# Two layer norms of a decoder layer, taken from sums and squares instead of transposes, and an up projection fed two tiles at a time

## The chip, the cores and the metric

The kernel runs on one core of a Trainium2 chip. The metric is the time of one execution on the device in microseconds (us). TensorE (PE) multiplies; VectorE (DVE), ScalarE (ACT) and GpSimd (POOL) do the elementwise work; SyncE (SP) issues most of the DMAs. Three runs of the kernel before took 1439.5 to 1440.29 us, median 1439.64.

## The reference

One decoder layer in fp32, for one prompt of 256 rows and eight sequences of four new rows each: 288 rows in all, model width 2048 (16 tiles of 128), FFN width 5504 (43 tiles).

```
shift1, scale1, gate1, shift2, scale2, gate2 = split(silu(c) @ w_ada + b_ada)
proj  = (x * (1 + scale1) + shift1) @ w_in            # q, k, v, u_a, v_a
mixed = concat(rms_norm(gated group), rms_norm(attention group))
x     = layer_norm(ALPHA * x + gate1 * (mixed @ w_out), ln1_g, ln1_b)
up    = (x * (1 + scale2) + shift2) @ w_up            # 86 tiles, then a causal conv of width 3
ff    = (silu(a) * b) @ w_down
y     = layer_norm(ALPHA * x + gate2 * ff, ln2_g, ln2_b)
# layer_norm(x): mu = mean(x); var = mean((x - mu)^2); (x - mu) * rsqrt(var + eps) * g + b
```

## The kernel before, in words

Everything lies with features on the partitions: xT holds x as 16 tiles of 128 features by 288 rows. So a layer norm's mean and variance run over partitions and tiles.

Weights stream through a ring of four slabs of 512 KB (raw). ScalarE copies a slab, rounded, to wH (`hi`, L920) and VectorE takes the remainder wL = raw - wH (`lo`, L1276). Activations are split in the same way (hH, hL), and each product is three matmuls (`products`, L444 to L446), 24 per slab. The semaphores split_done (slab ready) and used (slab consumed) order this; a slab is split three ahead of its use (AHEAD). Each engine's order is written out by hand, and each executes its list strictly in order, SyncE's queue of loads too.

The modulation (w_ada) is another stream: ada slabs in a ring of eight, multiplied in bursts of four between product slabs (`ada_next`, L460), copied by ScalarE (adaS, L932), transposed (`ada_turn`, L501) and added into modT by VectorE (`unit_finish`, L1290, L1494 to L1496). The last unit, U_SC2B, gives scale2 for the upper half of the tiles; its 16 ada slabs stand in the first norm.

Output projection, second half: four groups g of four output tiles, four slabs each (PSUM banks 0 to 3). When group g is done, `residual(g)` on VectorE adds gate times product to xT into S4 (L1649, L1650, L1654), and gives the banks back. ScalarE copies S4 to xT (`copy_sum`, L1149). TensorE transposes S4 into three banks (`turn_rows`, L750, 12 transposes), one group later, within the product loop, and VectorE takes bn_stats of the rows (L1660). After group 3, `normalise` aggregates, ScalarE takes the root (L1156), VectorE builds six diagonal matrices DG (L1677), and `spread_rows` multiplies ones by DG (L760) so that each row's 1/sd and -mean/sd stand on all partitions; they are copied to RN (L1158, L1682). `centre` applies them to four tiles at a time (L1688, L1689). In the first norm, per four tiles: H2 = x * scale2 + shift2 (ScalarE L1180 for the prompt, VectorE L1715, L1716 for the samples), hH (L1185), hL (L1722), and ScalarE's `affine` (L1166), which turns xT into the norm's output for the residual of the next norm. (ln1_g and ln1_b are folded into scale2 and shift2.)

Up phase: groups of eight slabs (`up_group`); each waits h2_ready for the four tiles that it reads. The first 32 slabs run in a loop of two with ada bursts (the last gate). Down projection: the last of three phases has groups of five and a half slabs, with the same residual, turn_rows and statistics. In the second norm VectorE centres tiles 0 to 11 and GpSimd tiles 12 to 15 (L1955, L1957), ScalarE applies g and b (L1166), and stores four tiles at a time (L1261).

## Time and profile before

| | us |
|---|---|
| median of three runs | 1439.64 |
| profiled execution | 1441.33 |
| its span | 1439.7 |
| TensorE busy | 1379.4 (96%) |
| VectorE busy | 843.0 (59%) |
| ScalarE busy | 571.5 (40%) |
| GpSimd busy | 109.6 (8%) |

The span runs from the first to the last instruction that the profiler saw; the execution's own time is 1.6 us longer. Busy shares are means over stages with different limits. Matmuls overlap in the pipeline, so a stretch in which TensorE is busy all the time isn't one at its peak. An fp32 matmul (not fp32r) is counted as two instructions, one per pass.

### The profile page before, as it was taken

How to read it: one execution, taken by the hardware profiler on the slowest of the kernel's cores; microseconds unless marked ns; L12 is line 12 of the kernel's file. 1: busy time of each engine (PE TensorE's matmuls, PEld its weight loads, DVE VectorE, ACT ScalarE, POOL GpSimd, SP SyncE). 2: the span in 40 equal slices, each digit the busy share in tenths (PEclk: the TensorE clock that was granted, in tenths of full speed). 3: DMA queues.
4: the chain of work that ended last, by engine and by line, in shares of the span. 5: the costliest groups of instructions: out<-in, count | busy, mean ns of one | idle time of the engine just before them, and what ended most of it. 6: DMA issues, size and time to landing. Idle time of an engine off the chain costs nothing.

```text
span 1439.7 us, 29195 instructions
## 1 busy us (share of the span) xinstructions
PE 1379.4 (96%) x11366; PEld 1307.1 (91%) x11366; DVE 843.0 (59%) x1375; ACT 571.5 (40%) x831; POOL 109.6 (8%) x252
## 2 busy tenths in 40 slices
PE   6999999999999998999999999999999999999992
PEld 5998888899788876989999999999999999999992
DVE  2476546558765456565667454675665445657555
ACT  3533222353533327443444333444444333444333
POOL 1000000003221000010101000010110000101002
PEclk9999999999999999999999999999999999999996
DMA  9989998974786985866554545445455444454621
GB/s 379 374 328 389 342 337 305 344 264 149 274 294 254 352 311 224 323 249 248 176 169 146 181 160 162 163 145 187 146 172 165 159 162 159 165 170 146 198 89 66
DMA packets 89183, 324.86 MB, mean 226 GB/s; under 512 B 10574, under 2 KB 10574, under 8 KB 88721
## 3 DMA queue, kind: packets, MB, share of 16 engines
q1 hardware_dynamic: 81216, 294.69, 57.5%
q0 software_dynamic: 6880, 24.10, 4.8%
q10 hardware_dynamic: 1008, 4.98, 0.9%
q8 instruction: 56, 0.92, 0.3%
q14 instruction: 23, 0.18, 0.0%
HBM read 318.05 MB, written 5.67 MB: 225 GB/s over the span
## 4 chain that ended last, share of the span: by engine, by line
PE 91%; DVE 4%; ACT 3%; issue 1%; DMA 1%; SPq 0%; ACTq 0%; DVEq 0%
PE ps L444 28%; PE ps L446 27%; PE ps L445 27%; PE ps L460 5%; ACT xT L1166 1%; DMA adaY<-w_ada 1%; PE ps L750 1%; PE ps L552 1%; DVE wL L1276 1%; DVE xT L1689 1%; DVE xT L1688 1%; ACT wH L920 1%; ACT H L1180 1%; PE ps L622 0%; PE ps L760 0%
## 5 line engine op out<-in xcount | busy, mean ns | idle before, releaser
L1276 DVE TENSOR_TENSOR wL<-raw,wH 128x1024 fp32r<-128x1024 f32 x372 | 448.7, 1216 | 375.9 <-ACT wH L920 373.2
L920 ACT ACTIVATE wH<-raw 128x1024 fp32r<-128x1024 f32 x372 | 389.5, 1053 | 602.5 <-PE ps L446 576.9
L444 PE MATMUL ps<-hL,wH 128*128 128x288 f32 x2016 | 603.5, 299 | 6.9 <-DVE hL L1314 4.0
L446 PE MATMUL ps<-hH,wH 128*128 128x288 f32 x2016 | 601.0, 298 | 0.0
L445 PE MATMUL ps<-hH,wL 128*128 128x288 f32 x2016 | 600.6, 298 | 0.0
L444 PEld LDWEIGHTS ps<-hL,wH 128*128 128x128 f32 x2016 | 381.5, 189 | 20.5 <-issue 8.9
L445 PEld LDWEIGHTS ps<-hH,wL 128*128 128x128 f32 x2016 | 381.1, 189 | 0.5 <-issue 0.5
L446 PEld LDWEIGHTS ps<-hH,wH 128*128 128x128 f32 x2016 | 380.2, 189 | 0.0
L444 PE MATMUL ps<-ffL,wH 128*128 128x288 f32 x688 | 204.4, 297 | 0.4 <-DVE xT L1769 0.3
L445 PE MATMUL ps<-ffH,wL 128*128 128x288 f32 x688 | 203.0, 295 | 0.0
L446 PE MATMUL ps<-ffH,wH 128*128 128x288 f32 x688 | 202.4, 294 | 0.0
L1455 DVE TENSOR_TENSOR proj<-ps,proj 128x288 f32<-128x288 f32 x160 | 71.0, 455 | 105.8 <-PE ps L446 105.3
L444 PEld LDWEIGHTS ps<-ffL,wH 128*128 128x128 f32 x688 | 128.9, 187 | 1.6 <-DVE xT L1769 1.5
L446 PEld LDWEIGHTS ps<-ffH,wH 128*128 128x128 f32 x688 | 129.6, 188 | 0.0
L445 PEld LDWEIGHTS ps<-ffH,wL 128*128 128x128 f32 x688 | 129.2, 188 | 0.0
L444 PE MATMUL ps<-mix,wH 128*128 128x288 f32 x256 | 80.0, 313 | 8.5 <-DVE xT L1541 4.3
L445 PE MATMUL ps<-mix,wL 128*128 128x288 f32 x256 | 77.2, 302 | 0.0
L446 PE MATMUL ps<-mix,wH 128*128 128x288 f32 x256 | 77.1, 301 | 0.0
L1933 POOL COPY E<-U 128x4 f32 (+1 forms) x44 | 9.0, 204 | 754.3 <-ACT U L1201 754.3
L444 PEld LDWEIGHTS ps<-mix,wH 128*128 128x128 f32 x256 | 49.7, 194 | 14.4 <-issue 9.5
L460 PE MATMUL ps<-ada,cT 128*32 128x256 f32 x832 | 51.7, 390 | 0.0
L445 PEld LDWEIGHTS ps<-mix,wL 128*128 128x128 f32 x256 | 49.9, 195 | 0.0
(230 smaller groups left out, 982.2 us busy)
## 6 DMA issues: line engine op xcount, KB each, us to landing
raw<-w_up SPq DMA_DIRECT2D x168, 512.0 KB, 3.5
ada<-w_ada SPq DMA_DIRECT2D x112, 512.0 KB, 6.2
raw<-w_down SPq DMA_DIRECT2D x84, 512.0 KB, 3.5
raw<-w_in SPq DMA_DIRECT2D x80, 512.0 KB, 7.9
adaX<-w_ada SPq DMA_DIRECT2D x40, 512.0 KB, 5.6
adaY<-w_ada SPq DMA_DIRECT2D x40, 512.0 KB, 7.4
raw<-w_out SPq DMA_DIRECT2D x32, 512.0 KB, 5.1
KV<-keys POOLq DMA_DIRECT2D x16, 512.0 KB, 5.8
```

Of the source, the lines that this page charges most:

```text
L444: nc.tensor.matmul(out, wH[:, w:w + P], rhs_lo(kk), start=start, stop=False)
L445: nc.tensor.matmul(out, wL[:, w:w + P], rhs_hi(kk), start=False, stop=False)
L446: mm = nc.tensor.matmul(out, wH[:, w:w + P], rhs_hi(kk), start=False, stop=stop)
L460: mm = nc.tensor.matmul(ps[32 * c:32 * c + 32, bank, 0:256], cT[:, 32 * k:32 * k + 32], src[:, 256 * c:256 * (c + 1)], start=(k == 0), sto ...
L552: mm = nc.tensor.matmul(b[:, lo:hi], ones[:, :], tile(proj, k0 + k, lo, hi), start=(k == 0), stop=(k == 7))
L750: mm = nc.tensor.transpose(b[0:n, t * P:(t + 1) * P], tile(S4, t, r * P, r * P + n), ident)
L920: nc.scalar.activation(wH[:, o:o + cols], raw[:, o:o + cols], ACT.Copy).then_inc(hi_done, 1)
L1166: y = nc.scalar.activation(tile(xT, k), tile(xT, k), ACT.Identity, scale=vec[:, scale_at + k:scale_at + k + 1], bias=vec[:, bias_at + k:bi ...
L1180: y = nc.scalar.activation(tile(H2, t, 0, SEQ), tile(xT, 4 * b4 + t, 0, SEQ), ACT.Identity, scale=modT[:, s:s + 1], bias=modT[:, c:c + 1])
L1276: vec_tt(wL[:, o:o + cols], raw[:, o:o + cols], wH[:, o:o + cols].bitcast(F32), ALU.subtract).then_inc(split_done, 1)
L1455: release(vec_tt(tile(proj, n), ps[:, k % 5, 0:ROWS], tile(proj, n), ALU.add), ("in", c, k))
L1688: steps.link(vec_tt(x, x, spread(RN[:, 0:1], [0, 4], [1, ROWS]), ALU.mult))
```

## The change

Both layer norms lose their transposes. After group 0's residual VectorE sums its four tiles per row (GS), one matmul of ones by GS (`centre_of`) gives the sum over the first 512 features on all partitions, and CM is that mean. It is subtracted from all tiles (`shift_group`), for groups 1 to 3 ahead of their residual. VectorE then gathers the sums (A1, `add_sum`) and the sums of ScalarE's squares (A2, `squares`, `add_squares`) of groups 0 to 2, one group later, by tensor_reduce over four tiles. `row_sums` on TensorE sums A1, A2, and the four tiles of group 3 and their squares over the partitions, with one moving column each: 10 x 3 matmuls, which give sums per row in six columns of a bank. From these come variance, root and mean in one column each; `spread_rows` multiplies that column, repeated 128 times as the stationary operand, by the identity, and `scaled` / `centred` read the result in PSUM. residual writes xT in place; S4 holds squares.

TensorE's order in the first norm: row_sums, eight ada slabs, spread_rows, four ada slabs, up slab 0, four ada slabs, up slab 1, the turn of U_SC2B, up slab 2 and on. The up phase waits for two tiles per slab; VectorE and ScalarE work in eight chunks of two tiles, with the splits of slabs S_UP+4 to S_UP+8 from chunk 3 on; the affine of xT moves behind, into slabs 8 to 15 of the up phase. The loop of two there is written out. In the second norm VectorE scales, ScalarE prepares WN = (-mean/sd) * g + b for each tile, VectorE forms x * g + WN, and SyncE stores two tiles at a time. GpSimd has no part in it. A one-column sqrt stands ahead of the last down phase.

```diff
+CM, _ = place("CM", [P, ROWS], over=o_cv)
+GS, _ = place("GS", [P, ROWS], over=o_cv + 4 * ROWS)
+A1, _ = place("A1", [P, ROWS], over=o_cv + 8 * ROWS)
+A2, _ = place("A2", [P, ROWS], over=o_cv + 12 * ROWS)
+TS, _ = place("TS", [P, 4 * SAMP], over=o_bd)
+WN, _ = place("WN", [P, T], over=o_h)
...
-    def turn_rows(g, ln):
...
+    def centre_of(ln):
+        pe.wait_ge(group_sum, ln + 1)
+        b = take(pe, ("centre", ln), 4)
+        fill(nc.tensor.matmul(b[:, 0:ROWS], ones[:, :], GS[:, :], start=True, stop=True), ("centre", ln))
+    def row_sums(ln):
+        pe.wait_ge(acc_ready, ln + 1)
+        b = take(pe, ("sums", ln), 5)
+        def add(src, at, first=False, last=False):
+            for r, lo in enumerate(ROW_BLOCKS):
+                mm = nc.tensor.matmul(b[:, at + r:at + r + 1], src[:, lo:lo + P], ones[:, 0:1], start=first and r == 0, stop=last and r == 2)
+            return mm
+        add(A1, 0, first=True)
+        add(A2, 3)
+        for t in range(4):
+            pe.wait_ge(d_ready, 7 * ln + 4 + t)
+            add(tile(xT, 12 + t), 0)
+            pe.wait_ge(squared, 7 * ln + 4 + t)
+            mm = add(tile(S4, t), 3, last=t == 3)
+        fill(mm, ("sums", ln))
     def spread_rows(ln):
-        pe.wait_ge(diag_ready, ln + 1)
+        pe.wait_ge(ln_root, ln + 1)
         for j in range(2):
+            if j == 1:
+                pe.wait_ge(mean_ready, ln + 1)
             b = take(pe, ("ln", ln, j), 4 + j)
             for r in range(3):
+                cols = ident if r < 2 else ident[:, P - SAMP:P]
                 n = P if r < 2 else SAMP
-                mm = nc.tensor.matmul(b[:, r * P:r * P + n], ones[0:n, :], DG[0:n, (2 * r + j) * P:(2 * r + j) * P + n],
+                mm = nc.tensor.matmul(b[:, r * P:r * P + n], spread(small[:, 142 + 3 * j + r:143 + 3 * j + r], [0, P]), cols,
                                       start=True, stop=True)
             fill(mm, ("ln", ln, j))
...
-            if g and j == 1:
-                turn_rows(g - 1, 0)
+            if g == 1 and j == 0:
+                centre_of(0)
     a = MOD_UNITS[U_SC2B][0]
-    for k in range(4):
-        ada_next(a + k)
-    turn_rows(3, 0)
-    for k in range(4, 8):
+    row_sums(0)
+    for k in range(8):
         ada_next(a + k)
     spread_rows(0)
-    for k in range(8, 16):
+    for k in range(8, 12):
         ada_next(a + k)
-    ada_turn(U_SC2B, ("turn", U_SC2B))
-    def up_group(s, i0, job, it, per, halves=2, units=None):
+    def behind_first(j):
+        if j == 0:
+            for k in range(12, 16):
+                ada_next(a + k)
+        if j == 1:
+            ada_turn(U_SC2B, ("turn", U_SC2B))
+    def up_group(s, i0, job, it, per, halves=2, units=None, behind=None):
         banks, deep = ([0, 1, 2, 3], 2) if halves == 2 else ([0, 2], 4)
         n = KT // deep
         for j in range(n):
-            pe.wait_ge(h2_ready, (j * deep + deep - 1) // 4 + 1)
+            pe.wait_ge(h2_ready, (j * deep + deep - 1) // 2 + 1)
             products(s + j, i0 + j, lambda kk: tile(hH, deep * j + kk), lambda kk: tile(hL, deep * j + kk),
                      banks, j == 0, j == n - 1, ktiles=deep, taking=lambda t: take(pe, (job, banks[t]), banks[t], it, per))
+            if behind is not None:
+                behind(j)
...
+            up_group(S_UP[0], 0, ("up", 0, "a"), 0, 2, units=0, behind=behind_first)
+            up_group(S_UP[0] + 8, 8, ("up", 0, "b"), 0, 2, units=0)
+            ada_turn(Q_UP, ("turn up", 0))
+            up_group(S_UP[0] + 16, 0, ("up", 0, "a2"), 0, 2, units=1)
+            up_group(S_UP[0] + 24, 8, ("up", 0, "b2"), 0, 2, units=1)
+            ada_turn(Q_UP + 1, ("turn up", 1))
...
+    for c in range(8):
+        sp.wait_ge(y_ready, c + 1)
+        sp.dma_start(io["yT"][:, c * 2 * ROWS:(c + 1) * 2 * ROWS], xT[:, c * 2 * ROWS:(c + 1) * 2 * ROWS]).then_inc(stored, 16)
+    sp.wait_ge(stored, 16 * 8)
...
+                if g and j == 2:
+                    squares(g - 1, 0)
+    def squares(g, ln):
+        act.wait_ge(d_ready, 7 * ln + g + 1)
+        nc.scalar.activation(tiles(S4, 0, 4), tiles(xT, 4 * g, 4), ACT.Square).then_inc(squared, 1)
     out_rest()
-    def normalise(ln, scale_at, bias_at):
-        copy_sum(3, ln)
+    def deviation(ln):
+        for t in range(4):
+            act.wait_ge(d_ready, 7 * ln + 4 + t)
+            nc.scalar.activation(tile(S4, t), tile(xT, 12 + t), ACT.Square).then_inc(squared, 1)
         act.wait_ge(ln_var, ln + 1)
-        nc.scalar.activation(small[:, 130:133], small[:, 126:129], ACT.Sqrt, bias=eps_col(1)).then_inc(ln_sd, 1)
...
+        nc.scalar.activation(small[:, 132:135], small[:, 129:132], ACT.Sqrt, bias=eps_col(1)).then_inc(ln_sd, 1)
+    deviation(0)
+    for c in range(8):
+        act.wait_ge(xn_ready, c + 1)
+        if c >= 2:
+            act.wait_ge(h2_ready, c - 1)
+        for t in range(1 if c == 0 else 2):
+            k = 2 * c + t
+            s, o = (SC2 + k) * MODS, (SH2 + k) * MODS
+            y = nc.scalar.activation(tile(H2, 2 * (c % 2) + t, 0, SEQ), tile(xT, k, 0, SEQ), ACT.Identity,
+                                     scale=modT[:, s:s + 1], bias=modT[:, o:o + 1])
+        y.then_inc(h2_prompt, 1)
+        act.wait_ge(h2_prompt, c + 1)
+        act.wait_ge(h2_32, c + 1)
+        nc.scalar.activation(tiles(hH, 2 * c, 2), tiles(H2, 2 * (c % 2), 2), ACT.Copy).then_inc(h2H, 1)
+        if c >= 3:
+            hi_ahead(S_UP[0], S_UP[0] // 4, c - 2)
+        if c == 3:
             unit_copy(U_SC2B)
-        act.wait_ge(xn_ready, b4 + 1)
...
+    def affine(c):
+        for k in (2 * c, 2 * c + 1):
+            y = nc.scalar.activation(tile(xT, k), tile(xT, k), ACT.Identity, scale=vec[:, V_G1 + k:V_G1 + k + 1],
+                                     bias=vec[:, V_B1 + k:V_B1 + k + 1])
+        y.then_inc(x1_ready, 1)
...
+            nc.scalar.activation(small[:, 135:136], eps_col(0), ACT.Sqrt)
...
+    deviation(1)
+    b = filled(act, ("ln", 1, 1))
+    for k in range(KT):
+        y = nc.scalar.activation(tile(WN, k), b[:, 0:ROWS], ACT.Identity, scale=vec[:, V_G2 + k:V_G2 + k + 1],
+                                 bias=vec[:, V_B2 + k:V_B2 + k + 1])
+        if k % 2:
+            y.then_inc(w_ready, 1)
...
     def residual(g, ln, job, gate_tile, td, s_last):
-        if ln or g:
-            dve.wait_ge(s4_copied, 4 * ln + g)
         for t in range(4):
             tile_filled(t, td, s_last)
-            n = gate_tile + 4 * g + t
...
+            n, k = gate_tile + 4 * g + t, 4 * g + t
+            part = vec_tt(by_seq(TS[:, t * SAMP:(t + 1) * SAMP].rearrange("p (k c) -> p k c", k=1), 1), by_seq(ps[:, t:t + 1, SEQ:ROWS], 1),
+                          mods(n, 1)[1], ALU.mult)
+            x = tile(xT, k, 0, SEQ)
+            if g == 3:
+                part.then_inc(part_done, 1)
+            release(vec_stt(x, ps[:, t, 0:SEQ], modT[:, n * MODS:n * MODS + 1], x, ALU.mult, ALU.add), job(t))
+            if g == 3:
+                dve.wait_ge(part_done, 4 * ln + t + 1)
+                vec_tt(tile(xT, k, SEQ, ROWS), tile(xT, k, SEQ, ROWS), TS[:, t * SAMP:(t + 1) * SAMP], ALU.add).then_inc(d_ready, 1)
+        if g < 3:
+            released(dve, job(3))
+            x = tiles(xT, 4 * g, 4, SEQ, ROWS)
+            ins = vec_tt(x, x, TS[:, :].rearrange("p (k c) -> p k c", k=4), ALU.add)
+            if g:
+                ins.then_inc(d_ready, 1)
+            else:
+                steps.link(ins)
+                nc.vector.tensor_reduce(GS[:, :], by_column(xT, 0), AX.X, ALU.add).then_inc(group_sum, 1)
+    def by_column(t, k):
+        return t[:, k * ROWS:(k + 4) * ROWS].rearrange("p (k c) -> p c k", k=4)
+    def shift_group(g):
+        x = tiles(xT, 4 * g, 4)
+        return vec_tt(x, x, spread(CM[:, 0:1], [0, 4], [1, ROWS]), ALU.subtract)
+    def centre_first(ln):
+        b = filled(dve, ("centre", ln))
+        release(vec_ts(CM[:, :], b[:, 0:ROWS], 1.0 / 512, None, ALU.mult), ("centre", ln))
+        released(dve, ("centre", ln))
+        shift_group(0).then_inc(d_ready, 1)
+        dve.wait_ge(group_sum, ln + 1)
+        steps.link(vec_stt(A1[:, :], CM[:, :], -4.0, GS[:, :], ALU.mult, ALU.add))
+    def add_sum(g, ln):
+        dve.wait_ge(d_ready, 7 * ln + g + 1)
+        steps.link(nc.vector.tensor_reduce(GS[:, :], by_column(xT, 4 * g), AX.X, ALU.add))
+        steps.link(vec_tt(A1[:, :], A1[:, :], GS[:, :], ALU.add))
+    def add_squares(g, ln):
+        dve.wait_ge(squared, 7 * ln + g + 1)
+        steps.link(nc.vector.tensor_reduce((GS if g else A2)[:, :], by_column(S4, 0), AX.X, ALU.add))
+        if g:
+            ins = vec_tt(A2[:, :], A2[:, :], GS[:, :], ALU.add)
+            if g == 2:
+                ins.then_inc(acc_ready, 1)
+            else:
+                steps.link(ins)
     def normalise(ln):
-        row_statistics(3, ln)
...
+        b = filled(dve, ("sums", ln))
+        release(vec_ts(small[:, 126:132], b[:, 0:6], 1.0 / D, None, ALU.mult), ("sums", ln))
+        released(dve, ("sums", ln))
+        steps.link(vec_tt(small[:, 145:148], small[:, 126:129], small[:, 126:129], ALU.mult))
+        vec_tt(small[:, 129:132], small[:, 129:132], small[:, 145:148], ALU.subtract).then_inc(ln_var, 1)
         dve.wait_ge(ln_sd, ln + 1)
-        steps.link(nc.vector.reciprocal(small[:, 142:145], small[:, 130:133]))
...
+        nc.vector.reciprocal(small[:, 142:145], small[:, 132:135]).then_inc(ln_root, 1)
+        dve.wait_ge(ln_root, ln + 1)
+        vec_stt(small[:, 145:148], small[:, 126:129], -1.0, small[:, 142:145], ALU.mult, ALU.mult).then_inc(mean_ready, 1)
+    def scaled(ln, c):
+        b = filled(dve, ("ln", ln, 0))
+        x = tiles(xT, 2 * c, 2)
+        steps.link(vec_tt(x, x, spread(b[:, 0:1], [0, 2], [1, ROWS]), ALU.mult))
+    def centred(c):
+        scaled(0, c)
+        b = filled(dve, ("ln", 0, 1))
+        x = tiles(xT, 2 * c, 2)
+        vec_tt(x, x, spread(b[:, 0:1], [0, 2], [1, ROWS]), ALU.add).then_inc(xn_ready, 1)
...
+            if g == 1 and j == 2:
+                centre_first(0)
+            if g and j == 3:
+                ins = shift_group(g)
+                steps.link(ins)
             out_step(16 + 4 * g + j)
-            if g and j == 2:
-                row_statistics(g - 1, 0)
+            if g >= 2 and j == 1:
+                add_sum(g - 1, 0)
+            if g and j == 3:
+                add_squares(g - 1, 0)
             if S_OUT + 16 + 4 * g + j in TURN_AT:
                 unit_finish(TURN_AT[S_OUT + 16 + 4 * g + j])
     normalise(0)
-    centre(0, 0)
...
+    centred(0)
+    for c in range(8):
+        x, samples = by_seq(tiles(xT, 2 * c, 2, SEQ, ROWS), 2), by_seq(tiles(H2, 2 * (c % 2), 2, SEQ, ROWS), 2)
+        dve.wait_ge(xn_ready, c + 1)
+        if c >= 2:
+            dve.wait_ge(h2_ready, c - 1)
+        if c == 0:
+            vec_ts(tile(H2, 1, 0, SEQ), tile(xT, 1, 0, SEQ), modT[:, (SC2 + 1) * MODS:(SC2 + 1) * MODS + 1],
+                   modT[:, (SH2 + 1) * MODS:(SH2 + 1) * MODS + 1], ALU.mult, ALU.add)
+        steps.link(vec_tt(samples, x, mods(SC2 + 2 * c, 2)[1], ALU.mult))
+        vec_tt(samples, samples, mods(SH2 + 2 * c, 2)[1], ALU.add).then_inc(h2_32, 1)
+        if c == 3:
             unit_finish(U_SC2B)
-        dve.wait_ge(h2H, b4 + 1)
-        vec_tt(tiles(hL, 4 * b4, 4), tiles(H2, 0, 4), tiles(hH, 4 * b4, 4).bitcast(F32), ALU.subtract).then_inc(h2_ready, 1)
+        if c < 7:
+            centred(c + 1)
+        dve.wait_ge(h2H, c + 1)
+        vec_tt(tiles(hL, 2 * c, 2), tiles(H2, 2 * (c % 2), 2), tiles(hH, 2 * c, 2).bitcast(F32), ALU.subtract).then_inc(h2_ready, 1)
+        if c >= 3:
+            lo(S_UP[0] + c - 2 + AHEAD, (c - 2 + AHEAD) % RING)
...
+    scaled(1, 0)
+    for c in range(8):
+        if c < 7:
+            scaled(1, c + 1)
+        dve.wait_ge(w_ready, c + 1)
+        for k in (2 * c, 2 * c + 1):
+            ins = vec_stt(tile(xT, k), tile(xT, k), vec[:, V_G2 + k:V_G2 + k + 1], tile(WN, k), ALU.mult, ALU.add)
+        ins.then_inc(y_ready, 1)
...
-    pool.wait_ge(s4_copied, 8)
...
```

## Rows read from the trace of the kernel before

**Rows 1.** Chain of waits (page, part 4): shares of the span by line.

```profile
PE ps L444 28%; PE ps L446 27%; PE ps L445 27%; PE ps L460 5%; ACT xT L1166 1%; DMA adaY<-w_ada 1%; PE ps L750 1%; PE ps L552 1%; DVE wL L1276 1%; DVE xT L1689 1%; DVE xT L1688 1%; ACT wH L920 1%; ACT H L1180 1%; PE ps L622 0%; PE ps L760 0%
```

**Rows 2.** Busy time by stage: stretch, length, each engine; clock, DMA share, GB/s.

```profile
488.20:506.60 18.40, 18.40 (x179) 16.18 (x175) 9.86 (x22) 5.68 (x6) 0.00 (x0) 1.00 0.91 346
536.15:551.40 15.25, 9.78 (x111) 5.31 (x110) 12.23 (x25) 6.68 (x13) 0.00 (x0) 0.89 0.96 361
1408.60:1439.70 31.10, 4.54 (x25) 3.58 (x24) 18.52 (x28) 11.89 (x20) 7.36 (x2) 0.62 0.19 76
```

**Rows 3.** The same view, single microseconds in which the clock falls.

```profile
542.00:543.00 1.00, 1.00 (x17) 0.49 (x20) 0.85 (x2) 0.00 (x0) 0.00 (x0) 0.63 1.01 410
1416.00:1417.00 1.00, 1.00 (x5) 0.94 (x5) 0.00 (x0) 0.41 (x1) 0.00 (x0) 0.53 0.00 0
```

**Rows 4.** TensorE by time, first norm: start, us, line, count [idle before].

```profile
488.20 1.53 PE L750 MATMUL ps<-cst,S 128*128 128x128 f32 x12
489.49 0.38 PE L444 MATMUL ps<-mix,wH 128*128 128x288 f32 x1
...
532.83 1.50 PE L460 MATMUL ps<-ada,cT 128*32 128x256 f32 x24
...
539.99 2.02 PE L760 MATMUL ps<-DG,ones 128*128 128x128 f32 x12 [1.90 <-DVE DG L1677]
541.94 3.39 PE L460 MATMUL ps<-ada,cT 128*32 128x256 f32 x32
...
551.06 0.44 PE L501 MATMUL ps<-cst,adaS 128*128 128x128 f32 x2 [3.34 <-ACT adaS L932]
551.45 0.39 PE L444 MATMUL ps<-hL,wH 128*128 128x288 f32 x1
...
566.03 1.93 PE L460 MATMUL ps<-ada,cT 128*32 128x256 f32 x32
570.42 0.40 PE L444 MATMUL ps<-hL,wH 128*128 128x288 f32 x1 [2.45 <-DVE wL L1276]
```

**Rows 5.** TensorE by time, second norm: its last product and the spread.

```profile
1408.40 0.29 PE L446 MATMUL ps<-ffH,wH 128*128 128x288 f32 x1
...
1415.33 2.92 PE L760 MATMUL ps<-DG,ones 128*128 128x128 f32 x12 [3.77 <-DVE DG L1677]
```

**Rows 6.** TensorE by time: sums over partitions, 256 and 32 moving columns.

```profile
418.42 3.72 PE L552 MATMUL ps<-proj,ones 128*128 128x256 f32 x16
...
458.33 1.87 PE L552 MATMUL ps<-proj,ones 128*128 128x32 f32 x16
460.13 0.64 PE L460 MATMUL ps<-ada,cT 128*32 128x256 f32 x8
```

**Rows 7.** VectorE by time around the last residual of the first norm.

```profile
529.74 0.29 DVE L1290 TENSOR_TENSOR modT<-ps,vec 128x36 f32<-128x36 f32 x2 [2.41 <-PE ps L501]
530.74 1.23 DVE L1276 TENSOR_TENSOR wL<-raw,wH 128x1024 fp32r<-128x1024 f32 x1 [0.71 <-ACT wH L920]
531.88 0.18 DVE L1649 TENSOR_TENSOR S<-ps,modT 128x32 f32<-128x32 f32 x1
...
532.38 0.18 DVE L1649 TENSOR_TENSOR S<-ps,modT 128x32 f32<-128x32 f32 x1
```

**Rows 8.** VectorE by time in the tail, beside GpSimd's L1955.

```profile
1420.24 3.65 DVE L1689 TENSOR_TENSOR xT<-xT,RN 128x1152 f32<-128x1152 f32 x1
```

**Rows 9.** Groups by form: count | busy us, mean ns | idle before.

```profile
L1740 DVE SCALAR_TENSOR_TENSOR CV<-U,cw,CV 128x304 f32<-128x304 f32 x86 | 42.3, 532 | 1.6
L1126 ACT ACTIVATE proj<-ps 128x288 f32<-128x288 f32 x40 | 15.5, 411 | 13.8 <-PE ps L446 13.7
L1722 DVE TENSOR_TENSOR hL<-H,hH 128x1152 fp32r<-128x1152 f32 x4 | 5.4, 1358 | 3.5 <-ACT hH L1185 3.4
L1584 DVE TENSOR_REDUCE small<-Ls 128x2 f32<-128x576 f32 x1 | 0.8, 753 | 0.0
```

**Rows 10.** ScalarE's queue by time: the last store.

```profile
1436.47 0.34 ACTq L1261 DMA_DIRECT2D yT<-xT  x1
```

More of the change, by code:

```diff
@@ L241, in decoder_layer_program @@
         S4, o_s4 = place("S4", [P, 4 * ROWS])
-        RN, _ = place("RN", [P, 2 * ROWS], over=o_s4)
         region = top
@@ L833, in _ @@
                                      taking=lambda t: take(pe, ("down", 2, g, t), t))
-                            if g and j == 2:
-                                turn_rows(g - 1, 1)
-                    turn_rows(3, 1)
+                            if g == 1 and j == 0:
+                                centre_of(1)
+                    row_sums(1)
                     spread_rows(1)
@@ L1214, in _ @@
                 if ph == 0:
-                    with act.Fori(0, 2) as u:
+                    for u in range(2):
                         for i in range(1, 17):
@@ L1218, in _ @@
                             if i == 16:
-                                act.wait_ge(bank_full[7], u + JOBS[("turn up",)][1])
+                                filled(act, ("turn up", u - 1) if u else ("turn", U_SC2B))
                                 ada_copy(u * 16 + (A_UP + 16))
@@ L1254, in _ @@
                                 hi(s, s // 4, s % 4, slab_columns(s))
[L1255 to L1262 removed]
+                            if g and j == 3:
+                                squares(g - 1, 1)
+            deviation(1)
[5 more added lines that the diff above has]
+                    y.then_inc(w_ready, 1)
         @block.vector
@@ L1686, in centre @@
-            def centre(b4, ln):
-                x = tiles(xT, 4 * b4, 4)
-                steps.link(vec_tt(x, x, spread(RN[:, 0:1], [0, 4], [1, ROWS]), ALU.mult))
-                vec_tt(x, x, spread(RN[:, ROWS:ROWS + 1], [0, 4], [1, ROWS]), ALU.add).then_inc(xn_ready, 1)
+                    n, k = gate_tile + 4 * g + t, 4 * g + t
+                    part = vec_tt(by_seq(TS[:, t * SAMP:(t + 1) * SAMP].rearrange("p (k c) -> p k c", k=1), 1), by_seq(ps[:, t:t + 1, SEQ:ROWS], 1),
+                                  mods(n, 1)[1], ALU.mult)
@@ L1776, in _ @@
                 if ph == 0:
-                    with dve.Fori(0, 2) as u:
-                        steps.enter(u, 9)
+                    for u in range(2):
                         for i in range(1, 17):
@@ L1822, in _ @@
                                 residual(g, 1, lambda t: ("down", 2, g, t), G2, TD_DN[2] + 3 * g, S_DN[2] + 6 * g + 5)
+                            if g == 1 and j == 2:
+                                centre_first(1)
+                            if g and j == 3:
+                                steps.link(shift_group(g))
                             if 0 < q < 24 - AHEAD:
                                 lo(s, s % RING, slab_columns(s))
-                            if g and j == 3:
-                                row_statistics(g - 1, 1)
+                            if g >= 2 and j == 1:
+                                add_sum(g - 1, 1)
+                            if g and j == 4:
+                                add_squares(g - 1, 1)
             normalise(1)
-            for b4 in range(3):
-                centre(b4, 1)
+            scaled(1, 0)
[6 more added lines that the diff above has]
+                ins.then_inc(y_ready, 1)
         @block.gpsimd
```

124 lines of the change are left out of this document (15 added, 109 removed).

## The prediction, made before the changed kernel was run

> **What bounds the kernel now.** I read the chain of waits first: 82% of it is the three product lines L444 to L446 on TensorE [rows 1]. So a cycle off VectorE or ScalarE is worth nothing by itself; time comes only from work taken off TensorE and from the places where TensorE stands. The busy time by stage shows them [rows 2]: between 488.2 and 506.6 us TensorE is busy all through; from 536.15 to 551.4 it works 9.78 of 15.25 us, around the first layer norm; after the last product, at 1408.6, 31.1 us pass with 4.54 us of TensorE. The reader should see in TensorE's own order of instructions what each hole waits for [rows 4]: 1.90 us for DG, 3.34 us for ScalarE's copy of adaS (queued behind an affine group), 2.45 us for the split of slab S_UP+4, which ScalarE can begin only when its whole norm is done. The granted clock is at its lower level (1.2 GHz) in part of these stretches [rows 3]: it fell at about 542.4, after TensorE had stood 1.9 us and then worked 2 us, and at about 1416.5 in the tail.
>
> **Transposes out, sums in, while products run (both norms).** turn_rows leaves the product loop three times in each norm. One costs TensorE 489.49 - 488.20 = 1.29 us from its first transpose to the next product [rows 4], on the path: 3 x 1.29 = 3.9 us each norm. centre_of comes in: one fp32 matmul of 288 columns. Sixteen passes of 256 columns took 3.72 us, 0.23 a pass [rows 6], so two passes are 0.5 us. It waits for GS. VectorE's residual of a group ends 1.7 us after the slab's end, and a tensor_reduce over 1152 elements follows; the nearest contiguous reduce took 0.753 us for 576 [rows 9], the nearest instruction of 1152 took 1.358 us. I take 1.36. GS is then ready about 3.1 us after the slab, while TensorE has a slab (3.2 us) and in norm 1 a burst in front of centre_of: hidden, with only some tenths to spare in norm 2.
>
> VectorE loses the row statistics (three bn_stats a group) and gains per group a shift (1.36), a sum (1.36 + 0.46) and a sum of squares (the same). That is cover as long as banks come free in time: residual(g) is now behind add_squares(g-1). For g=1 in norm 1 the order is unit_finish, shift 1.4, split 1.23 [rows 7], reduce 1.4, so residual starts 2.2 us after the slab's end and bank 0 is free at +2.8, against a need at +2.1 behind the burst: 0.7 us lost. For g=2 it just fits; in norm 2, without burst, I count 0.1. Sum: norm 1 -3.9 + 0.5 + 0.7 = -2.7; norm 2 -3.9 + 0.5 + 0.1 = -3.3 us. DMA is at a share of 0.91 in this stretch [rows 2]; a period shorter by 1.3 of 18.4 us takes it to 0.98, which still fits.
>
> **row_sums, the new item on the path.** Thirty fp32 matmuls whose moving operand is one column but whose stationary operand is 128 columns wide: 60 passes. The nearest row is L552 with 32 columns: 16 passes between 458.33 and the next work at 460.13, at most 0.113 each, 0.107 without the switch [rows 6]. L460 loads 32 columns and moves 256 at 1.93 / 32 = 0.06 a pass [rows 4], so the 128 loaded columns set the 0.107, and one moving column should cost the same. 60 x 0.107 = 6.4 us; TensorE needs 1.28 us per tile, more than VectorE's 0.6 (0.49 now [rows 7], plus the sample add) or ScalarE's square. Bounds: near zero if one column made a pass four times shorter (-4.8 us), 0.17 each at the lower clock (+3.8). This also holds the four ada slabs that stood in front of turn_rows.
>
> **Norm 1, from the end of the last product slab at 532.83 [rows 4].** VectorE: unit 9 done at 530.1 [rows 7], shift(3) to 531.5, split to 532.7, add_squares(2) to 534.6. That is acc_ready, so row_sums goes from 534.65 to 541.1; the dense work ended at 532.8, and with the clock falling as late after it as in the row (4.4 us), the last 36 passes cost up to 0.063 more each: 541.1 to 543.4. Eight ada slabs then stand in front of spread_rows: 0.47 each at the full level (1.93 us for four with the pipeline's end), 0.85 at the lower (3.39 us for four [rows 4]): to 544.8 or 548.7. Root and mean themselves are ready earlier (about 1.3 us after the sums), so the six small DG multiplies and two copies (RN) that go were worth nothing here. Spread, two halves of about 1 us [rows 4]: 546.8 / 550.7. First chunk: multiply and add of 576 elements (0.75 each [rows 9]; the multiply under the second half): 547.6 / 551.5; sample part 0.75, centred(1) 1.55, low part 0.75: up products start at 550.7 / 554.6, against 551.45 now. From there eight slabs at 3.22, four late ada slabs 1.9, the turn 0.4 and the burst 1.9 are 30.0 us. Does VectorE feed them? A chunk costs it 0.45 + 1.6 + 0.7 = 2.75 us, from c=3 on 4.0 with the split, against 3.2; it starts a chunk ahead, and ada work gives TensorE 3.8 us more to do, so it keeps up but for some tenths. The one new wait of size is VectorE's own: unit_finish(U_SC2B) in c=3 waits for a turn that stands behind slab 1, some 3 us; queued behind it are centred(4) and hL of chunk 3, which TensorE wants at that moment (0.2). The affine leaves ScalarE's norm; the split of S_UP+4 comes by 20 us after the first chunk and is wanted later: the 2.45 us hole [rows 4] goes. Slab 7 ends at 581 / 585.5 with a fall of the clock in the pause before the up products; now it is at 583.58, start of the next burst. I take 0 for this part (-2.5 to +2).
>
> **The tail, from 1408.4.** Now: after the last product at 1408.4 the after the last product at 1408.4 the spread starts at 1415.33 and takes 2.92 us [rows 5], and the end is a chain of 1152-element instructions, two of them held to 3.65 us beside GpSimd [rows 8], then four groups of affine and a DMA issued at 1436.47 [rows 10]. After: row_sums to 1414.8 (1416.0 with a clock fall); six small steps of some 0.2 to 0.35 us, 1.3 together, to 1416.1 / 1417.3; the spread's first half 1.46: 1417.6 / 1418.8; its second: 1419.0 / 1420.2. Two ScalarE tiles at 0.41 (L1126, the same 288 elements out of PSUM [rows 9]) give w_ready: 1419.9 / 1421.1. VectorE's chunk is a multiply of 576 (0.75) and two scalar_tensor_tensor of 288 (0.532 for 304, start to start 0.45 [rows 9]): 1.65; first pair 0.95, seven more 11.5 less the 0.8 that the last lacks: 1431.6 / 1432.8. The last DMA now ends 3.2 us after its issue starts with 576 KB; with 288 KB I take 2.5: 1434.1 / 1435.3, so -5.6 / -4.4, taken as -5.0. The new sqrt preload saves nothing: the table load stands beside bn_stats today.
>
> **Sum.** -2.7 + 0 - 3.3 - 5.0 = -11.0 us on a span of 1439.7: 1428.7; with the 1.6 us around the span (1441.33 against 1439.7) the profiled execution would give 1430.3. The median of the runs is 1439.64, so I take the same difference off that: 1429 us.
>
> **Where the Trainium skill speaks against it.** The six reduces of a norm read with a step of 288 floats; no row shows such a read on VectorE. The Trainium skill, page "SBUF — State Buffer", section "Door 1: The DMA port swizzle", says in its note on cachelines that accesses that leave a 16-byte line pay a penalty, so that fp32 strides freely only over four elements. It gives no figure. The mechanism is the first rival, priced from rows.
>
> **Rivals.** (a) The stepped reduces run at half rate: 2.56 us instead of 1.36. Each of them in front of a residual is on the path: norm 1 +1.2 (g=1), +0.9 (g=2), +1.2 (before acc_ready); norm 2 +0.7 (centre_of waits), +0.7, +1.25. Sum +6.0: 1435. For it: only the stride; against: every VectorE row here of fp32 runs at one element per cycle whatever its pattern of repeats.
> (b) The reduces at the worst rate of a 1152-element row, 3.65 us [rows 8]: +12.4, 1441, no change.
> (c) Slower: the two-tile chunks of the up phase run serially. VectorE and ScalarE hand each chunk to and fro; if nothing overlapped, 4.0 + 2.1 = 6.1 us per chunk, against TensorE's 4.1 (33 us for eight): +16 us, 1445. It decides from 1.4 us over TensorE's pace per chunk. Against it: centred(c+1) is issued ahead of the low part of c and fills ScalarE's time.
> (d) One-column passes are much cheaper than 0.107, or the clock holds: the better ends of both parts, -2.5 and -5.6 or beyond: 1425.
>
> **How the numbers follow.** The forecast with its clock cases (1425.5 to 1432) 0.62, (a) 0.15, (b) 0.05, (c) 0.06, (d) 0.12. A measurement here tells 0.2%, 2.9 us, from no change. (a) counts mostly as faster. Faster 0.86, same 0.07, slower 0.07. Range 1424 to 1436: it leaves out (b), (c) and the far end of (d).
>
> **What would show it.** L750 gone from the rows; between 488 and 530 a group period of about 17.1 instead of 18.4 us without TensorE idle; row_sums' 60 passes in 6 to 8 us in both norms (if in 2 us, or in over 10, that step is wrong); tensor_reduce of 1152 elements at 1.36 us (at 2.5, rival (a)); first up product within 2 us of 551.45 less 2.7; the eight up slabs in 30 to 31 us with TensorE idle under 1.5 us; scaled at 0.75 us without GpSimd; last DMA issue 23 to 25 us after the last product. The prediction is wrong if TensorE waits for VectorE in the product loops, or row_sums costs much other than 6.4 us.

## The result: no change, where 11 us less was forecast

The changed kernel takes 1443.39 us (median of 20 runs, 1440.78 to 1445.87); the kernel before takes 1440.44 us beside it (20 runs, 1439.22 to 1443.39). The ratio is 1.0014, 95% interval 1.0008 to 1.0021: less than the 0.2% named above, so no change by that measure, though the interval lies wholly on the slower side. The forecast was 1429 and the range ended at 1436. Single executions of one kernel differ by 4 to 5 us, so a profile is read by its stages and the verdict by medians.

The profiled execution took 1443.01 us, its span 1441.0. First the busy time by stage (stretch, length, busy time and instruction count of TensorE, its weight loads, VectorE, ScalarE, GpSimd; granted clock, DMA share, GB/s), for the three stretches that answer to [rows 2] and for the two stretches of row_sums:

```profile
488.05:506.60 18.55, 17.03 (x166) 14.86 (x162) 13.02 (x23) 5.55 (x7) 0.00 (x0) 1.00 0.95 362
535.13:557.46 22.33, 20.68 (x168) 16.35 (x169) 8.70 (x27) 4.05 (x9) 0.00 (x0) 0.69 0.35 129
1411.00:1441.00 30.00, 13.36 (x74) 13.14 (x72) 15.30 (x37) 9.66 (x21) 0.00 (x0) 0.54 0.21 79
...
535.13:547.08 11.95, 11.95 (x64) 11.94 (x68) 3.45 (x13) 1.78 (x4) 0.00 (x0) 0.55 0.00 0
1411.19:1421.60 10.41, 10.40 (x61) 10.31 (x59) 1.30 (x8) 1.33 (x4) 0.00 (x0) 0.61 0.00 0
```

The reader should see two things. In a group of the product loop TensorE now stands for 1.5 us where it was busy all through. And the sixty passes of row_sums take 11.95 and 10.41 us, not 6.4, at a mean granted clock of 0.55 and 0.61. TensorE by time shows them, and what follows up to the first product of the up phase:

```profile
535.13 1.71 PE L760 MATMUL ps<-ones,A 128*128 128x1 f32 x12 [2.39 <-DVE A L1729]
536.70 1.42 PE L760 MATMUL ps<-ones,xT 128*128 128x1 f32 x6
...
547.01 3.34 PE L464 MATMUL ps<-ada,cT 128*32 128x256 f32 x32
...
552.00 1.52 PE L781 MATMUL ps<-cst,small 128*128 128x128 f32 x12
...
557.46 0.40 PE L448 MATMUL ps<-hL,wH 128*128 128x288 f32 x1 [0.17 <-DVE hL L1801]
...
570.15 0.40 PE L448 MATMUL ps<-hL,wH 128*128 128x288 f32 x1 [0.54 <-DVE hL L1801]
...
588.42 1.93 PE L464 MATMUL ps<-ada,cT 128*32 128x256 f32 x32
```

Six passes start every 1.28 us, 0.213 a pass, where a pass took 0.107 in [rows 6]. In the second norm the same instructions show both prices, with no idle time ahead of them:

```profile
1412.29 0.81 PE L760 MATMUL ps<-ones,xT 128*128 128x1 f32 x6
1412.96 0.95 PE L760 MATMUL ps<-ones,S 128*128 128x1 f32 x6
1413.77 1.42 PE L760 MATMUL ps<-ones,xT 128*128 128x1 f32 x6
```

Six passes take 0.67 us from start to start, then 1.28; the granted clock goes from 1.00 to 0.50 at 1413.5, 2.5 us into the narrow passes. The up phase starts at 557.46 instead of 551.45 [rows 4]. VectorE's groups by form (count | busy us, mean ns | idle before) hold the other surprise, the tensor_reduce over 1152 elements with a step of 288:

```profile
L1721 DVE TENSOR_REDUCE GS<-xT 128x288 f32<-128x1152 f32 x4 | 9.1, 2271 | 0.0
L1727 DVE TENSOR_REDUCE GS<-S 128x288 f32<-128x1152 f32 x4 | 9.0, 2243 | 0.0
L1548 DVE TENSOR_REDUCE small<-Lp 128x1 f32<-128x256 f32 x8 | 3.3, 409 | 0.0
L1547 DVE TENSOR_REDUCE small<-Lp 128x1 f32<-128x128 f32 x8 | 2.3, 286 | 0.3
```

The wide ones take 2.24 to 2.27 us, against the 1.36 of the forecast. What TensorE waited for from 480 to 590 us (us in all, times, longest):

```profile
PE ps L760 <- DVE A L1729: 2.4, 1, 2.4
PE ps L448 <- DVE xT L1686: 2.4, 2, 1.5
PE ps L464 <- DMA ada<-w_ada: 1.5, 2, 0.8
PE ps L448 <- DVE hL L1801: 0.7, 2, 0.5
```

L1686 is the residual that frees a product bank. In the second norm, from 1325 to 1412 us, it costs another 1.7 us:

```profile
PE ps L448 <- DVE xT L1686: 1.7, 2, 1.1
PE ps L751 <- DVE GS L1698: 0.4, 1, 0.4
```

The chain of waits behind the last product, which starts at 1410.9 us (start, us, what):

```profile
1411.19 10.41 PE ps L760 x60
1422.78 2.78 PE ps L781 x12
```

### The profile page after: what moved, and what is told of

Same layout as the page of the kernel before. It is cut to its first block, busy times and chain, and to the rows that moved or that the text cites. A ratio compares the mean times of both kernels' runs of the same rounds, so it can differ in the third digit from the quotient of the medians.

```text
span 1441.0 us, 29173 instructions
## 1 busy us (share of the span) xinstructions
PE 1389.8 (96%) x11394; PEld 1318.2 (91%) x11394; DVE 869.5 (60%) x1412; ACT 568.1 (39%) x836; POOL 103.0 (7%) x250
## 4 chain that ended last, share of the span: by engine, by line
PE 92%; DVE 4%; ACT 1%; DMA 1%; issue 1%; SPq 0%; DVEq 0%; ACTq 0%
PE ps L448 28%; PE ps L450 27%; PE ps L449 27%; PE ps L464 5%; PE ps L760 2%; DMA raw<-w_in 1%; DVE wL L1310 1%; PE ps L556 1%; ACT wH L951 1%; PE ps L626 0%; DVE GS L1727 0%; DVE xT L1751 0%; DVE xT L1922 0%; PE ps L653 0%; SPq L882 0%
## 5 line engine op out<-in xcount | busy, mean ns | idle before, releaser
L448 PEld LDWEIGHTS ps<-mix,wH 128*128 128x128 f32 x256 | 49.7, 194 | 18.6 <-issue 13.6
L450 PEld LDWEIGHTS ps<-mix,wH 128*128 128x128 f32 x256 | 50.0, 195 | 0.0
```

The source lines that it names most:

```text
L448: nc.tensor.matmul(out, wH[:, w:w + P], rhs_lo(kk), start=start, stop=False)
L450: mm = nc.tensor.matmul(out, wH[:, w:w + P], rhs_hi(kk), start=False, stop=stop)
```

## The experiments

Three theories. **Theory 1**: in a run of products with one moving column the granted clock falls to its lower level (1.2 GHz), and each pass then costs double, in both norms on the path. **Theory 2**: the stepped reduces are slow, and stand on VectorE in front of the residuals and of acc_ready. **Theory 3**, the rival to both others: the two-tile feed, or the transfers of the modulation slabs, set the start of the up phase whatever the sums cost.

**Row sums as wide products.**

```diff
-                def add(src, at, first=False, last=False):
-                    for r, lo in enumerate(ROW_BLOCKS):
-                        mm = nc.tensor.matmul(b[:, at + r:at + r + 1], src[:, lo:lo + P], ones[:, 0:1], ...)
+                def add(bank, src, first=False, last=False):
+                    return nc.tensor.matmul(bank[:, 0:ROWS], ones[:, :], src, start=first, stop=last)
...
-                    spread_rows(1)
```

> The changed kernel, but row_sums multiplies an all-ones 128x128 weight by the 288 columns of each source (10 products of 288 columns) instead of each source by one column of ones (60 products of one column). The sums then stand in every partition, so the root chain runs on 128x288 tiles and spread_rows is gone. Theory 1 (the one-column products let TensorE's clock fall and so cost 0.17 to 0.20 us each instead of 0.107): each dense product takes 0.48 us and the granted clock holds, so the sums take 4.8 us instead of 11.95 in norm 1 and 10.4 in norm 2; the chain is 1 us longer, the spread (1.5 to 2.8 us) goes. First product of the up phase near 548 us instead of 557.5, last store 5 to 6 us earlier; 1428 us in all. Rival (TensorE's clock falls with any work of this kind, 0.96 us a product): sums still 9.6 us, 1439 us. Rival (the chunked feed sets the start of the up phase, not the sums): no gain in norm 1, 5 in the tail, 1438 us.

Measured: 1434.29 us, ratio 0.9955 (0.9942 to 0.9968) to the kernel before. TensorE by time, first and second norm:

```profile
535.37 1.24 PE L760 MATMUL ps<-A,ones 128*128 128x288 f32 x4 [2.39 <-DVE A L1713]
536.44 1.06 PE L760 MATMUL ps<-xT,ones 128*128 128x288 f32 x2
...
541.53 0.65 PE L760 MATMUL ps<-S,ones 128*128 128x288 f32 x2
...
550.44 1.08 PE L464 MATMUL ps<-ada,cT 128*32 128x256 f32 x8 [2.04 <-DMA ada<-w_ada]
...
1408.30 1.13 PE L760 MATMUL ps<-A,ones 128*128 128x288 f32 x4
1412.67 0.65 PE L760 MATMUL ps<-S,ones 128*128 128x288 f32 x2
```

In the second norm the sums take 4.9 us, as expected, and the end comes 25 us after the last product, not 30. In the first norm, behind the 2.4 us of idle time, the clock does fall at 536.5 us, for four products (0.85 to 0.96 us instead of 0.485 each), and comes back while the wide products run: 6.6 us. So the gain was 9 us and not 15. Two things were missed: the reciprocal of 288 columns takes 1.95 us, and with earlier sums the modulation slabs arrive too late. The edit changes the number of passes (60 to 20) as well as their width, so it fits theory 1 but doesn't isolate the clock; the filler run below does. Theory 3 holds in part, as the next bound.

**Modulation slabs around the narrow sums**: three of the eight slabs ahead of row_sums, four between its tiles.

```diff
-            row_sums(0)
-            for k in range(8):
+            for k in range(3):
+                ada_next(a + k)
+            row_sums(0, [a + 3, a + 4, a + 5, a + 6])
+            ada_next(a + 7)
```

> The changed kernel with only TensorE's order in norm 1 changed: 3 of the 8 modulation slabs stand ahead of row_sums (in the 2.4 us in which it waits for the accumulators), 4 between its tiles, 1 behind it. Theory 1: with wide products between them the one-column products take 0.107 us each, so sums and four slabs take 6.4 + 2.5 us, the spread starts near 545 instead of 552 and the up phase near 550.7 instead of 557.5: 1436.5 us. Rival (a one-column product costs 0.2 us whatever stands between): only the 2.4 us of waiting are filled, up phase near 555.5, 1441.5 us. Rival (feed bound): no change, 1443.4 us.

Measured: 1441.42 us, ratio 1.0003 (0.9994 to 1.0012); up phase from 557.20 us.

```profile
537.91 0.81 PE L760 MATMUL ps<-ones,S 128*128 128x1 f32 x6
538.65 0.64 PE L464 MATMUL ps<-ada,cT 128*32 128x256 f32 x8
539.22 0.93 PE L760 MATMUL ps<-ones,xT 128*128 128x1 f32 x6
540.01 1.42 PE L760 MATMUL ps<-ones,S 128*128 128x1 f32 x6
541.36 1.08 PE L464 MATMUL ps<-adaX,cT 128*32 128x256 f32 x8
```

The time is the first rival's, but its interval overlaps that of the changed kernel (1.0008 to 1.0021) and the up phase starts where it did, so the time separates nothing. The trace does: a pass costs about 0.11 us until the clock falls at 539.8, 4.0 us into the sums, and double from there, together with the slabs (0.64 to 1.08). The slabs are work, but they did not hold the clock. That asked for a cleaner test of what does.

**Wide products as mere filler**, in the second norm, result unread:

```diff
                 def add(src, at, first=False, last=False):
+                    if ln:
+                        nc.tensor.matmul(e[:, 0:ROWS], ones[:, :], A1[:, :], start=True, stop=True)
```

> The changed kernel with one extra product of 288 columns (all-ones weight by the accumulator, into an unused bank, result not read) ahead of each of the 10 groups of one-column products in the norm at the end. It adds 10 x 0.48 = 4.8 us of TensorE work. Theory 1 (the clock falls for want of dense work): the one-column groups fall to 0.64 us, the whole stretch takes 11.2 us or so instead of 10.4, the spread behind it 0.8 instead of 1.5 us; the kernel's time is unchanged within 1 us. Rival (one-column products cost 0.2 us by themselves): 10.4 + 4.8 = 15.2 us, the kernel 5 us slower.

Measured: 1445.40 us, ratio 1.0030 (1.0018 to 1.0043), whose interval overlaps that of the changed kernel (1.0008 to 1.0021). The median is 2 us above the forecast, and the profiled execution has 3.2 us more in its first two up stages, which the edit doesn't touch; so the sums themselves have to be read. The busy time in the stretch of the sums:

```profile
1416.35:1427.90 11.55, 11.55 (x82) 10.47 (x80) 1.46 (x8) 1.49 (x4) 0.00 (x0) 1.00 0.01 1
```

and TensorE's last pair by time:

```profile
1426.66 0.73 PE L762 MATMUL ps<-A,ones 128*128 128x288 f32 x2
1427.23 0.72 PE L764 MATMUL ps<-ones,S 128*128 128x1 f32 x6
```

This decides theory 1. The granted clock is 1.00 from end to end, a group of six narrow passes takes 0.57 to 0.59 us from its start to the next product, and 4.85 us of additional products made the stretch only 1.1 us longer (10.41 in the changed kernel). A narrow pass costs about 0.1 us at the upper level; the other half was the clock.

**One slab ahead of each tile group**, to see which work holds the clock:

```diff
                 def add(src, at, first=False, last=False):
+                    if slabs and not first and src is not A2:
+                        ada_next(slabs.pop(0))
```

> The changed kernel with one modulation slab (32 products with a 32-column weight and 256 columns, 0.62 us at the upper clock level) directly ahead of each of the eight tile groups of row_sums in norm 1, and none behind. Theory 1a (any wide product between the groups holds the clock, as the extra 288-column products with full weights did in the norm at the end): sums and slabs take 10 x 0.64 + 8 x 0.62 = 11.4 us, the spread starts near 546.5 instead of 552: 1438 us. Theory 1b (only products that fill the array count; four slabs between the groups did not hold the clock): the clock falls as before, about 17 us for the stretch: 1443 us, as changed.

Measured: 1449.18 us, ratio 1.0063 (1.0047 to 1.0080). Busy time in the whole stretch, then two pieces of it by time:

```profile
533.72:554.69 20.97, 20.97 (x124) 14.28 (x124) 3.44 (x13) 1.77 (x4) 0.00 (x0) 0.52 0.56 178
```

```profile
546.11 1.44 PE L764 MATMUL ps<-ones,xT 128*128 128x1 f32 x6
547.48 1.08 PE L464 MATMUL ps<-adaX,cT 128*32 128x256 f32 x8
```

TensorE is busy for all of 20.97 us and is granted 0.52. Theory 1b, and worse than it said: the slabs, which use a 32-column weight, are slowed as well. (A slab is four products, eight passes, as the rows show, and not the 32 that the forecast says.) With full 128-column weights and 288 columns in the same proportion the clock stayed at 1.00. The runs differ in idle time ahead too (2.4 us here, none there). For the narrow passes alone the second norm settles it: with no gap ahead, in this run, the changed kernel and the two with slabs or pairs of chunks, whose second norm is the same, the clock fell 2.4 to 3.6 us into them. For the alternation with slabs, the kind of work and the gap aren't separated: behind 1.0 us of idle time it lost the clock too, after 4.0 us, but no run has it with none.

**Contiguous additions for the stepped reduces**, all twelve of them:

```diff
-                steps.link(nc.vector.tensor_reduce(GS[:, :], by_column(xT, 4 * g), AX.X, ALU.add))
+                v = t[:, k * ROWS:(k + 4) * ROWS]
+                steps.link(vec_tt(half, v[:, 0:2 * ROWS], v[:, 2 * ROWS:4 * ROWS], ALU.add))
+                return vec_tt(out, Ff[:, 0:ROWS], Ff[:, ROWS:2 * ROWS], ALU.add)
```

> The changed kernel with each stepped tensor_reduce (128x288 from 128x1152, 2.06 to 2.26 us) replaced by two tensor_tensor adds on contiguous halves (576, then 288 elements; by like rows 0.7 + 0.4 us). Theory 2 (the long reduces delay the residuals and so the release of the banks): the 2.4 us of TensorE's waits for the residual in the loop of norm 1 and the 1.7 us in norm 2 go, and the accumulators are ready 1.1 us earlier before row_sums: 4 to 5 us off, 1439 us. Rival (the waits are for the shift and the order of VectorE's queue, not for the reduces' length): under 1.5 us off, 1442 us.

Measured: 1434.52 us, ratio 0.9955 (0.9941 to 0.9969): 9 us off the changed kernel, where 4 to 5 were expected. VectorE's first halves by form, TensorE's waits from 480 to 590 us, and the busy time in the two stretches of row_sums:

```profile
L1704 DVE TENSOR_TENSOR Ff<-xT 128x576 f32<-128x576 f32 x6 | 4.5, 753 | 0.1
```

```profile
PE ps L464 <- DMA ada<-w_ada: 1.7, 3, 0.7
PE ps L760 <- DVE A L1732: 1.5, 1, 1.5
PE ps L448 <- DVE xT L1686: 0.6, 1, 0.6
```

```profile
531.80:541.30 9.50, 9.50 (x60) 9.48 (x61) 3.44 (x13) 1.77 (x4) 0.00 (x0) 0.70 0.00 0
1402.24:1411.60 9.36, 9.36 (x62) 9.32 (x60) 1.46 (x8) 1.50 (x4) 0.00 (x0) 0.70 0.01 2
```

The wait for the residual fell from 2.4 to 0.6 us, and the 1.7 us in the second norm are gone. The loops can be timed to 0.02 us in every profile: in the first norm from a split of VectorE just ahead of the loop (475.95 us before, 476.65 after) to the last product of it 56.66 us before, 55.80 after, 53.95 here; in the second norm, from the first product of the last down phase to the last, 74.20, 73.51 and 71.01. What had not been expected is the second effect: in the first norm TensorE stands 1.5 instead of 2.4 us ahead of the sums, the clock falls 3.8 us into them instead of 1.1, and the same sixty passes take 9.5 us instead of 11.95. Four profiles with 2.4 us of idle time ahead of narrow sums show the fall after 0.7 to 1.2 us, the two with 1.5 and 1.0 us after 3.8 and 4.0; so the removed wait was most likely paid twice, once in itself and once in the clock. In the second norm that doesn't apply: nothing is idle ahead of the sums in either kernel, and the 1.05 us by which they are shorter are no more than the spread of four profiles whose second norm is that of the changed kernel (9.43 to 10.49 us). The sum, 1.85 + 2.5 in the loops, 0.9 of waiting, 2.45 + 1.05 in the sums, is 8.75 us. The stages give somewhat less: of the 3.35 us at the first norm's sums 2.3 reach the first product of the up phase, since the eight modulation slabs behind the sums take 5.8 us instead of 5.0, more of them at the lower clock.

**TensorE waits for pairs of chunks:**

```diff
-                    pe.wait_ge(h2_ready, (j * deep + deep - 1) // 2 + 1)
+                    pe.wait_ge(h2_ready, 2 * ((j * deep + deep - 1) // 4) + 2)
```

> The changed kernel, but TensorE's up phase waits for pairs of two-tile chunks, as it waited for groups of four tiles in the kernel before; everything else is as changed. Theory 3 (the finer feed buys the start of the up phase): the first product comes one chunk later, 2.3 to 3.1 us, and since TensorE bounds the stretch behind it the kernel is 2 to 3 us slower, 1446 us. Rival (the feed is hidden anyway, because the modulation slabs and their transfers fill the time until the second chunk): 1443.4 us, within 1.

Measured: 1448.02 us, ratio 1.0053 (1.0029 to 1.0077).

```profile
559.51 0.49 PE L448 MATMUL ps<-hL,wH 128*128 128x288 f32 x1 [2.58 <-DVE hL L1801]
...
573.72 0.61 PE L448 MATMUL ps<-hL,wH 128*128 128x288 f32 x1 [3.73 <-DVE hL L1801]
```

The interval lies above that of the changed kernel (1.0008 to 1.0021); the medians are 4.6 us apart, and 2.9 if each is taken against the kernel before measured beside it. In the trace TensorE waits 2.4 us more at the start and 3.2 more at slab 4, which agrees with a few microseconds and not with the 1 of the rival. So the finer feed is the part of the change that pays. As the rival to theories 1 and 2, theory 3 falls by this and by the wide sums, which moved the start of the up phase from 557.46 to 552.74 us with the same feed.

**Both edits together.**

> Both edits together: all-ones weights and 288-column products for the row sums, and two contiguous additions for each stepped reduce. Theories 1 and 2 as two separate costs: sums start near 531.8 us and take 4.9 us at the upper clock level, the root chain 4.5, the first chunk 3.7, so the up phase starts near 546.5 (557.5 in the changed kernel), norm 2's loop gains 2.5 us and the tail 5.5: 1425 us. Rival (both edits gave the same microseconds, because the short wait that the tree leaves already lets the clock hold longer, or because the transfers of the modulation slabs bound norm 1): 1430 to 1434 us.

Measured: 1427.33 us, ratio 0.9898 (0.9882 to 0.9915). It lies between the two forecasts and 2 us from the additive one. The sums now run at full clock, 0.485 us each, but a modulation slab comes late, and the up phase starts at 548.2 us:

```profile
537.09 0.65 PE L760 MATMUL ps<-S,ones 128*128 128x288 f32 x2
545.95 0.64 PE L464 MATMUL ps<-ada,cT 128*32 128x256 f32 x8 [2.06 <-DMA ada<-w_ada]
```

**The version with everything:** slabs ahead of and between the wide sums (their slots come free earlier), the last residual ahead of the last sum of squares, the last four squares in a buffer of their own, the mean subtracted while the squares are summed, and in the second norm ScalarE's gain and bias in place of WN. These steps weren't run apart, so their shares are not shown.

```diff
+            for k in range(2):
+                ada_next(a + k)
+            row_sums(0, [a + 2, a + 3, a + 4, a + 5])
...
                         residual(g, 0, lambda t: ("out", g, t), G1, TD_OUT_B + 3 * g, S_OUT + 19 + 4 * g)
+                        if g == 3:
+                            add_squares(2, 0)
...
+                shifted(0)
+                steps.link(shifted(1))
+                b = filled(dve, ("sqs", ln))
```

> As the one before, and: in norm 1 two modulation slabs stand ahead of the sums and four between them, the last residual goes ahead of the last sum of squares on VectorE, the four last squares go to a buffer of their own; the mean is subtracted before the root is known, then the root multiplied, and in the norm at the end ScalarE applies gain and bias in a pass of its own instead of preparing a product for VectorE. By the rows so far: sums done 6.5 us after the last product, up phase from 545.5 us; the tail behind the last product 22.8 us (29.8 in the changed kernel, 24.8 with dense sums alone): 1422 us. Rival (the clock falls at the idle time before the sums whatever they are made of): 3 us more, 1425. Rival (bound by transfers of the modulation slabs): up phase from 549, 1426 us.

Measured: 1423.34 us, ratio 0.9868 (0.9850 to 0.9885). No wait for a transfer or for the accumulators is left; TensorE stands 3.66 us for the first chunk, behind the root chain. The last run uses that hole: two more slabs ahead of the up phase.

```diff
-            for k in range(6, 12):
+            for k in range(6, 14):
```

> The version with everything, and two of the four modulation slabs that stand behind the first slab of the up phase moved ahead of it, into the 3.7 us in which TensorE waits there for the first chunk. If their transfers have landed by then (they are 1.3 us each, one behind the other, and the slots come free from 538 us), 1.2 us are saved: 1422 us. Rival (they land too late and TensorE waits for them instead of the chunk): 0 to 2 us lost, 1424 us.

Measured: 1420.08 us, ratio 0.9854 (0.9837 to 0.9870), 20 us or 1.5% under the kernel before. Its interval overlaps that of the version above, so the last step is likely, not shown. TensorE's two last pauses before the up phase, and the chain of waits behind the last product:

```profile
543.71 0.64 PE L464 MATMUL ps<-adaX,cT 128*32 128x256 f32 x8 [0.47 <-DMA adaX<-w_ada]
546.36 0.61 PE L448 MATMUL ps<-hL,wH 128*128 128x288 f32 x1 [2.01 <-DVE hL L1797]
```

```profile
1399.30 2.60 PE ps L760 x10
1402.91 1.43 DVE xT L1732 x2
1405.49 1.97 DVE GS L1745
```

From the last product to the end it takes 22.4 us (1399.0 to 1421.4), against 30.1 in the changed kernel and 31.3 before.

## Why the prediction was wrong, step by step

The stages of the two profiles, as far as the change touches them: the loop of norm 1 is 0.86 us shorter (forecast 2.7), from its last product to the burst behind up slab 7 it takes 55.97 us instead of 50.97 (forecast no difference), the loop of norm 2 is 0.69 us shorter (forecast 3.3), the rest behind the last product 1.2 us shorter (30.1 against 31.3; forecast 5.0). That is +2.25 us where -11.0 was forecast, and the medians differ by 2.95; the two profiles differ by 1.3 us, since the stages in between, which the change doesn't touch, also vary. Each of the four terms failed by its own step or by the same one twice:

- **Transposes out, both loops: forecast -2.7 and -3.3.** The counting was right to 0.1 us: with contiguous additions the loops are 2.71 and 3.19 us shorter than before. The step that failed is "a tensor_reduce over 1152 elements ... I take 1.36". At 2.26 us it held back the residuals: bank waits of 2.4 us instead of 0.7, and of 1.7 + 0.4 instead of 0.1 in the second. Rival (a) had the mechanism and nearly the size (2.56), and was given 0.15.
- **row_sums: forecast 6.4 us in either norm.** The 0.107 per pass was right as a price at the upper level: the filler run shows it. The failed step is the clock. "The last 36 passes cost up to 0.063 more each" stood only as an upper end in norm 1, and in the tail 1.2 us were allowed; measured are 5.5 and 4.0 us. The price at the lower level was too small as well: the 0.17 a pass of the bounds, 0.063 over the upper level, has no row behind it, and 0.213 was measured. The row used as a model, the sums over 32 columns, lasted 1.8 us, with other work on both sides [rows 6], and bore out nothing for a stretch four times as long. [Rows 3] showed the fall in the very places where the narrow work was put. And the forecast had the cheaper form at hand: it took centre_of, ones by 288 columns, at 0.5 us, and ten of those are 5.0 us, less than the 6.4 that it took for the sixty passes at the upper level.
- **Norm 1 around the sums: forecast 0 (-2.5 to +2), measured +5.0.** The up phase began at 557.46 against the bounds 550.7 and 554.6; it is the 5.5 us of the sums and 0.5 of acc_ready, less what the shorter stretch from there to the burst gives back (30.96 us against 32.13). The rest held: eight modulation slabs 4.99 us (forecast 3.7 to 5.3), 31.0 us to the burst (30.0), 0.7 us of waits at chunks; the 2.45 us for the split at 570 are gone, and 0.54 for hL stand there.
- **Tail: forecast -5.0, measured -1.2.** Root chain 1.2 us (1.3), spread 2.8 (2.9), chunks 1.64 (1.65), from the last chunk to the end 2.5 (2.5). What is missing, 3.8 us, is in the main the 4.0 us of the sums.

Rival (c), the slower case, fell: TensorE waits 0.7 us in all for chunks, and the run with pairs of chunks is slower. That the measured time came out nearest to rival (b), no change, is chance: its mechanism, reduces at 3.65 us, did not occur. Rivals (b) and (d) fell with the durations above. The chances went wrong because the clock was treated as a spread of a few microseconds inside the main case, with no rival of its own, though the two stretches in which it could act were the largest new items on the path.

The Trainium skill, page "SBUF — State Buffer", section "Door 1: The DMA port swizzle", warned of strides beyond 16 bytes in fp32. The trace agrees in direction: in one kernel contiguous reduces go from 286 to 409 ns for 128 more elements, 0.96 ns each, and the reduce with a step of 288 takes 2.26 us for 1152, 1.96 ns each. Whether it is the step or the 288 separate results was not tried.

## What to carry to other kernels

A sum over partitions is cheap with the ones as the weight and the data as the moving side: the product count falls, the result stands in every partition, and the granted clock held here, or came back during the sums where 2.4 us of idle time stood ahead. Price a run of narrow matmuls at both clock levels, even where nothing is idle ahead of it. Before a strided reduce goes ahead of anything that releases a bank, compare it with two contiguous additions.

## What the hardware showed that was not expected

- TensorE fully busy is not TensorE at full clock: 20.97 us without a gap were granted 0.52 when one-column groups alternated with 32-column weights, 11.55 us were granted 1.00 when they alternated with full-width products. One-column groups alone lost the clock 2.4 to 3.6 us in, straight behind dense products.
- The clock came back during the sums themselves once they were wide: 0.85 to 0.96 us a product until 540.0, 0.485 from there.
- The long stages have two lengths each, in kernels that don't differ in them: the second up stage (eight groups) took 204.9 us in some profiles and 206.6 in others, the third (five groups) 140.9 or 142.1. The kernel before had the long and the short one, the changed kernel the short and the long one. That alone makes single executions differ by up to 2.9 us; what selects the length is open.
- VectorE's reciprocal costs 1.95 us for 288 elements, four times an ordinary pass (0.46 us). In the narrow form it had cost 0.18 us for three, so the wide sums pay 1.8 us a norm for it, and still win.
- In the last version what bounds the first chunk is the chain variance, root, reciprocal, 3.0 us behind the last sum of squares. A shorter root was not tried.
